# Hybrid decoder block, last third: output projection by token tiles, residual sums on VectorE, second norm by tiles

## What is computed

```python
h = RMSNorm(x) * norm_mix_w
p = h @ w_in                                  # q/k/v/z/gates of two mixers
A = gated_delta_rule(p); B = forgetting_attention(p)
y = sigmoid(gA) * (A @ w_branch_a) + sigmoid(gB) * (B @ w_branch_b)
x = x + y @ w_out
x = x + (silu(h2 @ w_gate) * (h2 @ w_up)) @ w_down   # h2 = RMSNorm(x) * norm_ffn_w
out = RMSNorm(x) * norm_final_w
```

## Time and profile before

| | us |
|---|---|
| median of 3 runs | 1137.33 (1137.09 to 1137.5) |
| profiled execution, whole | 1137.37 |
| its span, first to last instruction | 1135.6 |

### The profile page before, as it was taken

The page is one execution under the profiler, slowest core; times in us unless marked ns, Lnnn a source line. Parts: engine busy times, 40 slices in busy tenths (PEclk is TensorE's granted clock), DMA queues, the critical chain, the costliest instruction groups (busy, mean ns, idle before and its releaser), DMA issues.

```text
span 1135.6 us, 16426 instructions
## 1 busy us (share of the span) xinstructions
PE 1125.8 (99%) x5917; PEld 943.8 (83%) x5917; DVE 543.5 (48%) x1148; ACT 454.3 (40%) x747; POOL 538.5 (47%) x326
## 2 busy tenths in 40 slices
PE   9999999999999999999999999999999999999997
PEld 7788888888888888888888888887888888888886
DVE  5666456465646347777777564323333333320001
ACT  6465443435343365555555422234222322221112
POOL 5345674433524266555555544434444444444443
PEclk9999999999999999999999999999999999999999
DMA  7233333231313254444444373423333333322231
GB/s 211 76 93 94 100 105 103 66 102 57 95 54 104 79 163 115 123 118 121 125 128 115 102 252 94 126 81 93 92 92 95 107 94 92 93 92 93 93 111 74
DMA packets 176179, 119.94 MB, mean 106 GB/s; under 512 B 6657, under 2 KB 164466, under 8 KB 176130
## 3 DMA queue, kind: packets, MB, share of 16 engines
q1 hardware_dynamic: 163088, 98.20, 30.1%
q10 hardware_dynamic: 13042, 21.07, 5.7%
HBM read 110.83 MB, written 8.42 MB: 105 GB/s over the span
## 4 chain that ended last, share of the span: by engine, by line
PE 98%; DVE 1%; DMA 1%; ACT 0%; POOL 0%; SPq 0%; DVEq 0%; issue 0%
PE ps L1579 70%; PE ps L2009 10%; PE ps L1693 7%; PE ps L1539 4%; PE ps L1901 2%; PE ps L1872 1%; PE ps L1871 1%; DMA x_nat<-in_x 1%; PE ps L1945 1%; PE ps L1629 0%; PE ps L1641 0%; PE ps L1700 0%; PE ps L1652 0%; DVE mixT L1530 0%; PE ps L1552 0%; DVE tmp L1486 0%
## 5 line engine op out<-in xcount | busy, mean ns | idle before, releaser
L569 POOL TENSOR_TENSOR w_lo<-raw,w_hi 128x1024 fp32r<-128x1024 f32 x169 | 414.4, 2452 | 512.4 <-ACT w_hi L723 512.4
L1579 PE MATMUL ps<-h_hi,w_hi 128*128 128x512 f32 x976 | 384.2, 394 | 0.0
L1579 PE MATMUL ps<-h_lo,w_hi 128*128 128x512 f32 x976 | 382.9, 392 | 0.0
L1579 PE MATMUL ps<-h_hi,w_lo 128*128 128x512 f32 x976 | 382.9, 392 | 0.0
L723 ACT ACTIVATE w_hi<-raw 128x1024 fp32r<-128x1024 f32 x169 | 179.3, 1061 | 487.2 <-PE ps L1579 377.9
L1579 PEld LDWEIGHTS ps<-h_hi,w_lo 128*128 128x128 f32 x976 | 183.3, 188 | 38.1 <-issue 0.7
L1579 PEld LDWEIGHTS ps<-h_hi,w_hi 128*128 128x128 f32 x976 | 183.4, 188 | 37.8 <-issue 0.5
L1579 PEld LDWEIGHTS ps<-h_lo,w_hi 128*128 128x128 f32 x976 | 183.5, 188 | 36.1
L1128 DVE SCALAR_TENSOR_TENSOR tmp<-ps,prm,tmp 128x511 f32<-128x511 f32 (+2 forms) x72 | 53.9, 749 | 48.4 <-ACT tmp L770 46.6
L1082 DVE TENSOR_SCALAR ms<-ss 128x1 f32<-128x1 f32 x8 | 1.2, 153 | 123.7 <-ACT raw L1055 117.4
L1495 DVE TENSOR_TENSOR f_lo<-tmp,f_hi 128x512 f32 (+1 forms) x22 | 40.5, 1842 | 33.6 <-ACT f_hi L1028 33.6
(11 more groups left out here) (282 smaller groups left out, 1579.2 us busy)
## 6 DMA issues: line engine op xcount, KB each, us to landing
raw<-in_w_in SPq DMA_DIRECT2D x79, 512.0 KB, 3.9
raw<-in_w_gate SPq DMA_DIRECT2D x22, 512.0 KB, 3.7
raw<-in_w_up SPq DMA_DIRECT2D x22, 512.0 KB, 3.8
raw<-in_w_down SPq DMA_DIRECT2D x22, 512.0 KB, 3.4
gate_dram<-gate ACTq DMA_DIRECT2D x24, 256.0 KB, 2.0
cum<-cum_dram ACTq DMA_DIRECT2D x8, 512.0 KB, 7.4
raw<-in_w_branch_a SPq DMA_DIRECT2D x8, 512.0 KB, 4.1
raw<-in_w_branch_b SPq DMA_DIRECT2D x8, 512.0 KB, 4.0
```

Source lines behind the costliest of these rows:

```text
L569: pool.tensor_tensor(w_lo[:, r % 2, :], raw[:, r, :], w_hi[:, r % 2, :], ALU.subtract)\
L1579: return pe.matmul(ps[:, bank, :], wts[wl][k], acts[xl][:, k, :], start=(n == 0), stop=(n == len(PASSES) - 1))
```

## The change

In words, engine by engine:

- **PE, output projection.** `w_out` is taken by row tiles k (as `w_down` was), tokens stationary, into all eight banks. The first `HELD` = 2 row tiles use the slots of `w_hi`/`w_lo` and run over all banks (24 matmuls each). The other six are split into `held_hi`/`held_lo`, six tiles in buffers of the branch operands `a_hi`, `b_hi`, `a_lo`, `b_lo`, and are then run bank by bank: 18 matmuls for one token tile and half, eight times. `unit_done` jumps by 7 after k = 1.
- **Residual.** `x2_half` on DVE adds the bank to `x_res` in place, for both sums. The transposing matmuls `residual`, `x2_turn` and those in `down(1)` are gone, and `x2T` too.
- **Second norm.** For each token tile: ACT squares two halves, DVE makes the mean in two steps (`row_mean2`), POOL the power, DVE multiplies by it and by the norm weight (held in `gate` for every partition, a new load of 512 KB issued by SP ahead of the gates of the merge), PE turns the tile in eight transposes (`h_turn`), ACT and DVE split it. `wide_row` and `rstdb` are gone.
- **PE, first two FFN units.** They are cut in two: 384 columns (three token tiles), then the 128 columns of the last tile, with the turning of the last tile between.
- **FFN.** SiLU reads PSUM; DVE multiplies PSUM by it. The two scalings are gone.
- **The last two down tiles** (k = 20 and 21) are taken together, bank by bank.
- **The end.** x2_half, half squares, mean, power and final product, one token tile after the other on DVE.

```diff
+        HELD = 2
+        held_hi, held_lo = ([t[:, :, :].rearrange("p (u a) n -> p u (a n)", a=2)[:, u, :] for t in pair for u in range(4)]
+                            for pair in ((a_hi, b_hi), (a_lo, b_lo)))
+        w_ffn = gate[:, :, :].rearrange("p a n -> p (a n)")
...
             sp.wait_ge(b_low, led(b_low, FH // 2))
+            sp.dma_start(w_ffn, norm_ffn_w[0].partition_broadcast(P)).then_inc(wffn_loaded, 16)
             load_gates(0)
...
-            for j in range(KT):
-                high_ahead(OUT0 + j // 4, j % 4)
-                act.wait_ge(unit_done, OUT0 * 4 + j + 1)
-                act.activation(h_hi[:, j, :], ps[:, j % 4, :], ACT.Copy,
-                               scale=prm[:, NFFN + j:NFFN + j + 1]).then_inc(h_high, 1)
+            for k in range(HELD, KT):
+                act.wait_ge(w_loaded[k % 4], 16 * (OUT0 + k // 4) + 16)
+                if k == HELD:
+                    act.wait_ge(unit_done, OUT0 * 4)
+                act.activation(held_hi[k - HELD], raw[:, k % 4, :], ACT.Copy).then_inc(w_high, 1)
+            for r in range(2):
+                high_part(FFN0, r)
...
+            for t in range(TT):
+                for a in range(2):
+                    x2_half(0, t, a)
+                row_mean2(0, t)
+                dve.wait_ge(rstd_ready, TT + t + 1)
+                for a in range(2):
+                    cols = slice(a * 512, (a + 1) * 512)
+                    dve.scalar_tensor_tensor(out=gin[:, t % 2, a, :], in0=x_res[:, t, cols], scalar=rstd[:, t:t + 1],
+                                             in1=w_ffn[:, cols], op0=ALU.mult, op1=ALU.mult).then_inc(x_scaled, 1)
+                for a in range(2):
+                    tile = h_hi[:, 4 * a:4 * a + 4, t * P:(t + 1) * P].bitcast(F32)
+                    dve.wait_ge(h_high, KT + 2 * t + a + 1)
+                    dve.tensor_tensor(h_lo[:, 4 * a:4 * a + 4, t * P:(t + 1) * P], bank4(2 * t + a), tile, ALU.subtract)\
+                        .then_inc(h_low, 1)
...
+            for t in range(TT):
+                for a in range(2):
+                    x2_half(1, t, a)
+                row_mean2(1, t)
+                dve.wait_ge(rstd_ready, 2 * TT + t + 1)
+                dve.scalar_tensor_tensor(out=x_res[:, t, :], in0=x_res[:, t, :], scalar=rstd[:, t:t + 1], in1=wfin,
+                                         op0=ALU.mult, op1=ALU.mult).then_inc(fin_ready, 1)
...
+            pe.wait_ge(y_low, led(y_low, KT))
+            for t in range(TT):
+                for n in range(2):
+                    for k in range(HELD, KT):
+                        if (t, n) == (0, 0):
+                            pe.wait_ge(w_low, OUT0 * 4 + k + 1)
+                        if t > 0 and (n, k) == (1, 4):
+                            h_turn(t - 1)
+                        for p in range(3):
+                            last = out_product(t, n, k, p)
+                    last.then_inc(out_done, 1)
...
+            most, rest = slice(0, (TT - 1) * P), slice((TT - 1) * P, T)
+            pe.wait_ge(h_low, KT + 2 * (TT - 1))
+            ffn_part(0, most)
+            h_turn(TT - 1)
+            ffn_part(1, most)
+            pe.wait_ge(h_low, KT + 2 * TT)
+            ffn_part(0, rest).then_inc(unit_done, 1)
+            ffn_part(1, rest).then_inc(unit_done, 1)
+            for r in range(2, 4):
+                unit(FFN0, r, h_hi, h_lo)
...
+            for t in range(TT):
+                for n in range(2):
+                    for k in range(FT - 2, FT):
+                        if (t, n) == (0, 0):
+                            pe.wait_ge(w_low, 4 * DOWN0 + k + 1)
+                        for p in range(3):
+                            last = down_product(k, t, n, p)
+                    last.then_inc(down_done, 1)
```

More of the change, by code:

```diff
@@ L1969, in _ @@
-            for j in range(KT):
-                if j >= 4:
-                    pe.wait_ge(h_low, KT + j - 3)
-                    pe.wait_ge(x2_copied, j - 3)
-                unit(OUT0 + j // 4, j % 4, y_hi, y_lo, [x2_turn(j - 1), residual(j)] if j else [residual(j)],
-                     None if j else (y_low, led(y_low, KT)), (19, 22) if j else (22,))
-            def wide_row():
-                pe.wait_ge(diag_ready, 1)
-                pe.matmul(ps[:, 4, :], step[:, 4 * P:5 * P], tmp[:, 0, :], start=True, stop=True)\
-                    .then_inc(wide_done, 1)
@@ L1981, in ffn @@
-            def ffn(i, first=False):
-                for r in range(4):
-                    if not first:
-                        s = ffn_up if r % 2 else ffn_scaled
-                        pe.wait_ge(s, led(s, i * 2 + r // 2 - 1))
-                    tasks = ([x2_turn(KT - 1)], [wide_row], [], [])[r] if first else ()
-                    unit(i + FFN0, r, h_hi, h_lo, tasks, (h_low, 2 * KT) if first and r == 0 else None,
-                         (20,) if r else (16,))
-            pe.wait_ge(h_low, 2 * KT - 1)
@@ L1991, in _, with out_product, h_turn @@
-            pe.wait_ge(x2_copied, KT - 1)
-            ffn(0, True)
+            def out_product(t, n, k, p, first=False):
+                acts = (y_hi, y_hi, y_lo)[p]
+                wts = (w_hi, w_lo, w_hi)[p][:, k, :] if k < HELD else (held_hi, held_lo, held_hi)[p][k - HELD]
+                return pe.matmul(ps[:, 2 * t + n, :], acts[:, k, t * P:(t + 1) * P], wts[:, n * 512:n * 512 + 512],
+                                 start=first, stop=(k == KT - 1 and p == 2))
+            def h_turn(t):
+                for a in range(2):
+                    pe.wait_ge(x_scaled, TT + 2 * t + a + 1)
+                    for k in range(4):
+                        last = turn(ps[:, 2 * t + a, k * P:(k + 1) * P], gin[:, t % 2, a, k * P:(k + 1) * P])
+                    last.then_inc(h_turned, 1)
@@ new lines, in ffn, with ffn_part @@
+            def ffn(i):
+                for r in range(4):
+                    s = ffn_mul if r % 2 else ffn_gate
+                    pe.wait_ge(s, led(s, i * 2 + r // 2 - 1))
+                    unit(i + FFN0, r, h_hi, h_lo)
+            def ffn_part(r, cols):
+                pe.wait_ge(w_low, 4 * FFN0 + r + 1)
+                for n, (wl, xl, k) in enumerate(PASSES):
+                    last = pe.matmul(ps[:, r, cols], slot(r)[wl][k], (h_hi, h_lo)[xl][:, k, cols], start=(n == 0),
+                                     stop=(n == len(PASSES) - 1))
+                return last
@@ L2021, in _, with down_product @@
-            pe.wait_ge(ffn_scaled, led(ffn_scaled, FT))
-            pe.wait_ge(ffn_low, led(ffn_low, FT - 2))
-            for k in range(FT):
-                if k == FT - 2:
-                    pe.wait_ge(ffn_low, led(ffn_low, FT))
-                down(k)
+            def down_product(k, t, n, p):
+                xt, wt = ((f_hi, w_hi), (f_hi, w_lo), (f_lo, w_hi))[p]
+                return pe.matmul(ps[:, 2 * t + n, :], xt[:, k, t * P:(t + 1) * P], wt[:, k % 2, n * 512:n * 512 + 512],
+                                 start=(k == 0 and p == 0), stop=(k == FT - 1 and p == 2))
```

195 lines of the change are left out of this document (80 added, 115 removed).

## The result

The changed kernel takes 1146.29 us (median of 4 runs, 1145.81 to 1146.55), the kernel before in the same session 1137.21 (1136.91 to 1137.5). The ratio is 1.0079 with an interval of 1.0062 to 1.0097: slower by 9.1 us. The profiled execution is the one of 1145.81 us, with a span of 1144.0; before it was 1137.37 and 1135.6.

The account below looks back on a forecast made before the run. PE, busy 99% of the span, was taken as the bound, with its feeding engines' timeline deciding. Terms -0.6 + 3.0 - 3.5 + 3.2 + 4.95 = +7.05 on 1137.37 gave 1144.4 us, range 1140.5 to 1149.

Parts of the forecast that it names:

- three signs of being wrong: Gaps absent, final products under 3.5 us apart, or granted clock under 1.00 between 712 and PE's end.
- rival C: PE's clock falls to 1.2 GHz in a new gap: +3.1 us, 1147.5; chance 0.20.
- The output projection: Matmuls 43.5, six transpose groups 2.8, waits for POOL's splits 3.9: 50.2 us, -0.6.
- The first FFN units: Two units cut into 384 and 128 columns, then the third unit's wait of 1.26: 15.9 us, +3.0.
- FFN and down tile 0: DVE loses two operations per channel tile, but PE does not wait there: 0.
- Down tile 1: Its eight groups of transposes go: 8.94 to 5.44 us, -3.5.
- The last two down tiles: PE waits for tile 21, wanted 0.68 us after tile 19 but ready after 3.9: +3.2.
- The end: DVE's serial 4.4 us per token tile ends 8.85 us behind PE instead of 3.9: +4.95.
- The new load: Norm weight load on SP's queue ahead of the merge gates: taken as 0, with 0 to +1.5 us.
- rival D: The norm weight load ahead of the merge gates costs its 1.5 us: 1145.9; chance 0.08.
- Rival A: PE's list alone decides, feeding engines staying hidden: -6.3 us, 1131.1; chance 0.06.
- Rival B: The end is as fast as before, DVE's steps overlapping: without the 4.95, 1139.4 us; chance 0.05.

Follow-up runs that it names:

- e1: Changed kernel with DVE's end skewed: sums of token tile t+1 before the final product of tile t; median 1143.99 us (1140.21 to 1145.93).
- e2: Changed kernel with down tiles 20 and 21 one after the other instead of as a pair; 1146.2 us.
- e4: Changed kernel with all eight w_out tiles held, loads issued earlier, tiles 0 and 1 run in two pairs of token tiles; 1142.76 us.
- e5: Changed kernel with transposes of zeros ahead of the projection's waits for held tiles 5, 6 and 7; 1145.28 us, median of three runs.
- e6: Changed kernel with the first two FFN units whole (512 columns), behind the fourth token tile's turning; 1150.44 us.
- e7: Kernel before with only its last two down tiles taken as a pair, bank by bank; 1142.09 us, ratio 1.0041.
- e9: Changed kernel with down tile 20 split into its own buffer and tile 21 in the slot of tile 18; 1142.49 us.
- e11: Changed kernel with the small FFN norm weight load at the program's start put back; 1146.05 us in one run.
- g1: Changed kernel with eight w_out tiles held, third FFN tile and down tile 20 in a spare buffer, DVE's end skewed; 1132.79 us, ratio 0.9963 to before.

## Why the prediction was right, and where it was off

The time was 1146.29 against 1144.4, inside the range, slower as forecast. Of the prediction's own three signs of being wrong, two stayed away: the gaps are there, and the final products stand 4.19 apart, not under 3.5. The third came true: the granted clock was 0.94 in the projection, because rival C happened beside the forecast. By its steps:

**The output projection was mis-sized.** The forecast said -0.6 (43.5 + 2.8 + 3.9 = 50.2); measured is +1.98. Of the difference 1.97 is the clock's fall (50.80 in e1 without it, 52.77 with it). The prediction had this as rival C, with the right place ("PE works only 0.68 in every 2.4") but a chance of 0.20 and a price of 3.1. It fell in the profiled run here, in the profiled ones of e2, e4, e5, e6, e7, e9 and e11 too, at one or more places, and by their granted clocks in most of the other runs. The price was less than 3.1: of 12 slow matmuls nine count, at 0.20 more each. What misled was to look for the longest gap. A single wait of 2.9 left the clock at 1.00 here, and the short ones of 0.97 and 1.34 with three matmuls between did not. With the projection's waits unfilled, the clock fell there in five of six profiled runs, so 0.20 was too low. The Trainium skill (TensorE: Matmul & The Clock Gate, "HAM oscillation — how this bites in real kernels") describes short bursts of matmuls between waits for an operand, with PE back at half clock after each wait. Its waits last 3 to 5 us, though, and the two here 0.97 and 1.34; the trace agrees on the pattern, with 0.50 in two windows of 3 us, and goes beyond the page in how short the waits were. The other 0.6 is POOL's: its six splits take 14.7 us from start to end, here (716.17 to 730.88) as in e1, and not 14.2, because the first two are slow beside DVE, and they begin 0.1 later. What follows the last wait takes as long as forecast (32.1 us in e1). The three gaps ended by POOL are there as said: 3.7 us in e1, 3.0 here, where the slow matmuls filled part of them.

**The first FFN units** are 15.68 (15.9 forecast). 384 columns follow at 0.173 and 128 columns at 0.111, as taken from the earlier trace rows; the third unit waits 0.98 (1.26). The figure of about 81 ns a matmul in the Trainium skill (TensorE: Matmul & The Clock Gate, "Back-to-back issue gap") is not borne out: it is 0.111 here, with fresh fp32r weights for each.

**FFN and down tile 0**: 0 forecast, +0.33 measured; it lies in the first matmuls behind the third unit's wait (0.34 and some at 0.235) and in the first of tile 0.

**Down tile 1**: -3.50, exact.

**The last two down tiles**: +3.24 for +3.2; e7 shows the same 3.1 in the kernel before.

**The end**: +4.30 for +4.95. DVE's period is 4.19, not 4.4; three times 0.21 is the difference. The second of two sums starts about 0.6 behind the first, not 0.73, and the next tile's first sum 1.20 behind the final product's start, not 1.27. The mechanism is shown by e1.

**The new load**: 0 as taken; rival D falls (0.57 us idle was left).

Rival A (PE's list alone, 1131.1) needed every feeding engine hidden. That is what g1 built, and it gives 1132.79. Rival B fell with the 8.26 us from PE's last product to DVE's.

The misses are -0.6, +2.6, -0.2, +0.3, -0.1 and -0.65, in all +1.35. That the total is off by only 1.35 is in part luck: the projection's +2.6, most of it a rival that the forecast had not booked, was half cancelled by the start's -0.6, which has no known cause, and the end's -0.65.

## What to carry to other kernels

Work taken off the full engine is worth its time only where its feeders keep pace: compare, at each place that becomes shorter, the feeder's time per tile (here 2.4 to 2.5 us on POOL) with the new time per tile on PE (0.68), and give the feeder buffers and an earlier start in the same change. At the end of a program the milestone is the first finished tile plus the slowest engine's period times the tiles left, so skew that engine's list. Where PE is full otherwise, count a wait not at its length alone but with a possible fall of the clock behind it, about 2 us here; runs of one kernel that spread over several us, the slower ones at lower granted clocks, as in e1, are its sign.
